# Loras moved between the tile products of a hybrid encoder's projection, in 64-column halves

## The chip, the cores and the metric

The kernel runs on one core of one Trainium2 chip. The metric is device time in microseconds (us) of one execution; medians of several runs are compared. All data are 32-bit floats.

## What is computed

The reference is one step of a streaming encoder layer. The part that matters here is the input side of the token mixer, for 2048 prompt tokens and 8 x 16 sample tokens (17 tiles of 128):

```python
h = rmsnorm(x, w) * (1 + sc1) + sh1          # sc1, sh1 and four more rows from silu(c) @ w_ada + b_ada
proj = h @ w_in                              # q, f, i, gate of the HGRN2 heads; r, k, v of the RWKV-7 heads
dh = shift_right(h, h_prev) - h              # the previous token's row, less this one's
xw, xa, xg = h + dh * mu[0], h + dh * mu[1], h + dh * mu[2]
w_pre = w0 + tanh(xw @ w1) @ w2              # w1: 1024 x 64
a = sigmoid(a0 + (xa @ a1) @ a2)             # a1: 1024 x 64
g = sigmoid(xg @ g1) @ g2                    # g1: 1024 x 128, g2: 128 x 512
```

Behind it stand two recurrences over the tokens, an output product, a router and a mixture of 32 experts.

## The kernel before, in words

`project` (L131) is the first of four parts that run one after another (`project`, `recur`, `merge`, `experts`). Each engine has its own program there, and all order between them is written out with semaphores (`ev(name)`). It has three stages.

**First stage, the tile loop** (TensorE L461 to L472, ScalarE L618 to L625, VectorE L814 to L826). For tile m, TensorE turns tile m+1 (`turn`, L425: eight transposes into banks 0 and 1), multiplies tile m by the 512 columns of i (`i_columns`, L435: eight products of 128 x 512, two instructions each, since a 32-bit product takes two passes; banks 2 and 3 in turn) and then does one of sixteen steps of the late modulation (`late_modulation`, L447, four products of 32 columns side by side into bank 4; `modulation`, L412). ScalarE and VectorE each scale and shift half of the turned tile into `hT` (`keep_h`, L600 and L789), prepare tile m+2 (`norm`, L587 and L782), and ScalarE copies the i product of tile m-1 to `stage` (`keep_i`, L609). POOL loads the modulation's weights two ahead (L266 to L274), and before the ninth of them the three lora weights `lora_w` (L268 to L271). SyncE loads x and stores i.

**Second stage, the loras.** It has 40 steps (g, k): five groups g (four of 512 tokens, one of the 128 sample tokens) by eight blocks k of 128 features. For a step n = 8 g + k, ScalarE writes three copies of h times (1 - mu) (`scale_h`, L630), VectorE adds the previous token's h times mu to each (`mix_h`, L828), and TensorE multiplies the three by w1, a1 and g1 and sums over k in PSUM (`lora`, L479). The mixed data have three buffers (`mixed`, L189), so scaling of step n waits until TensorE is done with step n-3 (L634). The two 64-column products go beside each other into one bank, the 128-column one into another, and two pairs of banks take turns by group:

```python
            def lora(g, k):
                low, high = (P[5], P[6]) if g % 2 == 0 else (P[7], P[4])
                for j in range(2):
                    eng.matmul(low[64 * j:64 * j + 64, 0:w], lora_w[:, k, 64 * j:64 * j + 64], mixed[:, n % 3, j, 0:w], start=(k == 0), stop=(k == KD - 1))
                eng.matmul(high[:, 0:w], lora_w[:, k, 128:256], mixed[:, n % 3, 2, 0:w], start=(k == 0), stop=(k == KD - 1)).then_inc(ev("mixed_used"), 1)
```

When a group is summed, ScalarE moves its two banks to `te` (`keep_lora`, L642: two sigmoids and a copy), VectorE turns the first into a tanh (L841), and TensorE makes the gate g of four tiles (`gate`, L490, one product of 128 x 512 each, banks 2 and 3 in turn) behind k = 5 and 6 of the next group. ScalarE copies all 17 gates to the two buffers of `stage` (`keep_gate`, L651), each when SyncE's store of the gate two before it has landed (`store_gate`, L361). TensorE waits for the last of these copies (L513 to L516) and goes on to the third stage.

**Third stage, the pairs** (L538): 20 pairs of a 128-feature block c and 448 tokens, with products for r, k, v, q and f and, for the first 13, one tile of the output gate with `wt`. POOL loads `wt` and the first five weight blocks `wc` in this order once the first stage is done (L275 to L282).

## Time and profile before

| | |
|---|---|
| median of three runs | 2957.2 us (2951.2 to 2960.57) |
| the profiled execution's own time | 2960.53 us |
| its span, first to last instruction | 2958.6 us |
| TensorE (PE) busy | 2727.0 us, 92% |
| VectorE (DVE) busy | 1521.0 us, 51% |
| ScalarE (ACT) busy | 847.7 us, 29% |
| GpSimd (POOL) busy | 351.7 us, 12% |
| mean granted TensorE clock | 0.968 of full speed |

The profiled execution is 3.3 us above the median. In the profile, PE is TensorE's products and PEld its weight loads, which run beside them; the ends of products are modelled, so starts are the better measure. A timeline row gives start and length in us, engine, line, operation, output and inputs, shape and count; in brackets the idle time before it and what ended it. Shapes like 128*64 are the rows and columns of TensorE's array that the weights take.

### The profile page before, as it was taken

What the parts mean: (1) busy time and instruction counts of PE and PEld (TensorE: products, weight loads), DVE (VectorE), ACT (ScalarE), POOL (GpSimd) and SP (SyncE); (2) the same over time, 40 slices, a digit from 0 to 9 for tenths busy, and PEclk for the clock granted to TensorE, in tenths of its full rate; (3) what the DMA queues carried; (4) which work ended last, traced back from release to release, by engine and by line L of the source; (5) the groups of instructions that cost most, each with busy time, mean ns of one, the idle gap of its engine ahead of it and who ended that gap; (6) DMA issues with size and microseconds to landing.
All of it is one profiled execution on the core that took longest, in us unless ns stands there. A gap on an engine that the chain in (4) does not pass through costs nothing. (4 is left out here: it accounts for less than half of the span.)

```text
span 2958.6 us, 80057 instructions
## 1 busy us (share of the span) xinstructions
PE 2727.0 (92%) x33313; PEld 1714.7 (58%) x33314; DVE 1521.0 (51%) x3704; ACT 847.7 (29%) x1747; POOL 351.7 (12%) x477
## 2 busy tenths in 40 slices
PE   6998999999999989999999699976999999999988
PEld 2432445455454547887878455543666667666753
DVE  3246356556666656777777445454333333333328
ACT  2347334333444433444444222220000000000006
POOL 0000000000000000211213000001122222222223
PEclk9999999999999989999999799997999999999999
DMA  8641024223232286665563586571798668778768
GB/s 300 215 151 43 31 91 136 92 101 128 101 122 92 94 262 155 163 187 157 151 180 117 171 289 224 221 277 62 274 377 325 238 252 328 277 293 321 294 211 342
DMA packets 307723, 580.29 MB, mean 196 GB/s; under 512 B 56494, under 2 KB 240742, under 8 KB 292168
## 3 DMA queue, kind: packets, MB, share of 16 engines
q1 hardware_dynamic: 257544, 486.12, 46.4%
q0 software_dynamic: 18736, 70.27, 6.7%
q10 hardware_dynamic: 31248, 21.08, 2.4%
q8 instruction: 150, 2.46, 0.3%
q14 instruction: 45, 0.37, 0.0%
HBM read 411.77 MB, written 165.60 MB: 195 GB/s over the span
## 5 line engine op out<-in xcount | busy, mean ns | idle before, releaser
L523 PE MATMUL pj_P<-normed,pj_wc 128*128 128x448 f32 (+2 forms) x1600 | 594.9, 519 | 0.9 <-ACT pj_stage L656 0.9
L2699 PE MATMUL moe_PG<-wgu,moe_xT 128*32 128x256 f32 x9600 | 557.1, 381 | 37.0 <-DVE moe_hid L2553 18.3
L2699 PEld LDWEIGHTS moe_PG<-wgu,moe_xT 128*32 128x32 f32 x9600 | 381.4, 110 | 192.7 <-issue 61.7
L523 PEld LDWEIGHTS pj_P<-normed,pj_wc 128*128 128x128 f32 x1600 | 295.8, 190 | 259.6 <-issue 243.6
L2710 PE MATMUL moe_PTY<-wd,moe_hT 128*32 128x256 f32 x4800 | 295.2, 379 | 4.5 <-DVE moe_hT L2556 4.4
L2598 ACT ACTIVATE moe_sg<-moe_PG 128x128 f32<-128x128 f32 x150 | 41.6, 277 | 828.2 <-PE moe_PG L2699 648.7
L2539 DVE STREAM_TRANSPOSE moe_xT<-moe_xg 128x256 f32<-128x256 f32 x151 | 98.6, 653 | 321.8 <-PE moe_PG L2699 315.6
L2132 PE MATMUL merge_PO<-merge_w,merge_mT 128*128 128x512 f32 x544 | 239.7, 599 | 0.8 <-DMA merge_w<-in_w_out 0.5
L2710 PEld LDWEIGHTS moe_PTY<-wd,moe_hT 128*32 128x32 f32 x4800 | 193.3, 110 | 75.3 <-DVE moe_hT L2556 7.6
L2638 POOL DMA_INDIRECT moe_xg<-scratch_h,moe_row x152 | 148.2, 975 | 570.9 <-DVE moe_xT L2539 562.5
L2132 PEld LDWEIGHTS merge_PO<-merge_w,merge_mT 128*128 128x128 f32 x544 | 102.6, 191 | 125.2 <-issue 124.5
L2535 DVE COPY moe_y<-moe_PTY 128x256 f32<-128x256 f32 x151 | 64.0, 424 | 186.7 <-DMA scratch_y_rows<-moe_y 145.8
L444 PE MATMUL pj_P<-pj_wt,normed 128*128 128x512 f32 x272 | 120.4, 596 | 0.0
L282 POOL DMA_DIRECT2D pj_wc<-in_w_in x20 | 17.6, 883 | 676.7 <-PE pj_P L525 640.0
L554 PE MATMUL pj_P<-pj_wt,normed 128*128 128x512 f32 x208 | 92.7, 599 | 0.0
L1808 DVE COPY_PREDICATED re_Y<-re_const,re_P 128x256 f32<-128x256 uint32 x166 | 64.4, 441 | 52.4 <-PE re_P L1339 49.8
L908 DVE SCALAR_TENSOR_TENSOR pj_lf<-pj_P,pj_z 128x448 f32<-128x448 f32 (+1 forms) x20 | 12.2, 611 | 151.4 <-ACT pj_z L715 151.4
L677 ACT ACTIVATE pj_rk<-pj_P,pj_keep_mu 128x448 f32<-128x448 f32 (+1 forms) x60 | 35.5, 601 | 184.2 <-DVEq L950 91.6
L838 DVE SCALAR_TENSOR_TENSOR pj_hk<-normed,pj_prm,pj_hk 128x512 f32<-128x512 f32 x96 | 65.5, 745 | 39.7 <-ACT pj_hk L639 39.4
L2246 DVE TENSOR_TENSOR merge_x<-merge_PO,merge_maps 128x1024 f32<-128x1024 f32 x17 | 20.8, 1225 | 124.8 <-PE merge_PO L2132 124.8
L444 PEld LDWEIGHTS pj_P<-pj_wt,normed 128*128 128x128 f32 x272 | 50.7, 192 | 58.3 <-issue 58.3
L958 DVE TENSOR_TENSOR pj_hk<-pj_hk 128x224 f32<-128x224 f32 (+2 forms) x240 | 71.6, 375 | 2.9
(428 smaller groups left out, 4007.3 us busy)
## 6 DMA issues: line engine op xcount, KB each, us to landing
wgu<-in_w_gate SPq DMA_DIRECT2D x32, 2048.0 KB
wgu<-in_w_up SPq DMA_DIRECT2D x32, 2048.0 KB
wd<-in_w_down SPq DMA_DIRECT2D x32, 2048.0 KB
scratch_y_rows<-merge_zeros SPq DMA_DIRECT2D x51, 512.0 KB, 5.0
scratch_hk<-pj_hk SPq DMA_DIRECT2D x16, 1344.0 KB, 5.8
normed<-scratch_hk SPq DMA_DIRECT2D x32, 640.0 KB, 8.0
re_hkf<-scratch_hk SPq DMA_DIRECT2D x32, 640.0 KB
scratch_y_rows<-moe_y ACTq DMA_DIRECT2D x604, 32.0 KB
```

The costliest lines, as they stand in the source:

```text
L444: ins = eng.matmul(P[2 + m % 2][:, :], hT_cols(m)[:, k, :], wt[:, k, :], start=(k == 0), stop=(k == KD - 1))
L523: ins = eng.matmul(bank[:, 0:wp], wc[:, j, k, :], hT[:, k, k0:k0 + wp], start=(k == 0), stop=(k == KD - 1), skip_group_check=True)
L554: ins = eng.matmul(PQ[:, :], rows[:, k, :], wt[:, k, :], start=(k == 0), stop=(k == KD - 1))
L838: ins = eng.scalar_tensor_tensor(out, before, prm[:, p:p + 1], out, ALU.mult, ALU.add)
L958: step(eng.tensor_tensor(d, d, s, ALU.mult))
L1808: eng.copy_predicated(every_other(Y[lv - 1], g), level_mask(C_LEVEL_T, lv).bitcast(U32).unsqueeze(1).to_broadcast([128, 4, CH]), heads(src ...
L2132: ins = eng.matmul(PO[:, half, :], mT[:, n % 2, k, :], w[:, k, 512 * half:512 * half + 512], start=(k == 0), stop=(k == KD - 1))
L2535: eng.tensor_copy(y[p][:, :], PY[:, :]).then_inc(ev("y_kept"), 1)
L2539: eng.transpose(xT[:, :, :], xg[p][:, :].rearrange("p (i k) -> p k i", k=KD)).then_inc(ev("xT_made"), 1)
L2638: eng.indirect_dma_start(xg[p][:, :], None, t["h2"].rearrange("t (q c) -> (t q) c", q=4), bass.IndirectOffsetOnAxis(ap=row[:, p:p + 1], ax ...
L2699: ins = eng.matmul(PG[32 * q:32 * q + 32, 0, 0:256].rearrange("p (a b) -> p a b", a=2), xT[:, k, :], wgu[p][:, :, k, 128 * q:128 * q + 128 ...
L2710: ins = eng.matmul(PY[32 * n:32 * n + 32, :], hT[:, k, :], wd[p][:, k, 256 * n:256 * n + 256], start=(k == 0), stop=(k == KE - 1))
```

## The change

- TensorE multiplies by g1 in two halves of 64 columns, so that all four products of a lora step have 64 columns. All four prompt groups use banks 5 and 6, the sample group 7 and 4.
- Steps 0 to 25 of the 40 stand in the tile loop: two behind each tile's product from tile 4 to tile 16. ScalarE scales them in tile m's part behind `keep_i(m - 1)`, VectorE mixes them at the end of its part. Steps 26 to 39 stay behind the loop, scaled and mixed two steps ahead of their use.
- The first two groups are moved to `te` as plain copies at tiles 8 and 12, and their sigmoids are done at once at tile 15 (`squash_early`). Group 2 is moved at tile 16.
- Of the gates, two follow each of the steps 26 to 31, and one each of the last four. Even ones are copied by ScalarE, odd ones by VectorE.
- POOL loads the lora weights ahead of the third modulation load, and the first r weights ahead of the gate weights.

```diff
+        EARLY_GROUPS = LORA_GROUPS - 2
+        EARLY = 512 * EARLY_GROUPS
+        N_LORA = KD * (LORA_GROUPS + 1)
+        FIRST_LATE = 2 * (NT - 4)
...
+        def lora_steps(m):
+            return range(2 * (m - 4), 2 * (m - 4) + 2) if m >= 4 else ()
+
+        def lora_banks(g):
+            return (P[5], P[6]) if g < LORA_GROUPS else (P[7], P[4])
+
+        def lora_gates(n):
+            if n < KD * LORA_GROUPS:
+                return range(2 * (n - FIRST_LATE), 2 * (n - FIRST_LATE) + 2)
+            return range(12 + n - (N_LORA - 4), 13 + n - (N_LORA - 4)) if n >= N_LORA - 4 else ()
+
+        def keep_gate(eng, m):
+            eng.wait_ge(ev("gate_made"), m + 1)
+            p = (NT + m) % 2
+            eng.wait_ge(ev(f"stage_out{p}"), 16 * (len(range(p, NT, 2)) + len(range((NT + p) % 2, m, 2))))
+            src, done = P[2 + m % 2][:, :], ev(f"gate_kept{m % 2}")
+            if m % 2 == 0:
+                eng.copy(stage[:, p, :], src).then_inc(done, 1)
+            else:
+                eng.tensor_copy(stage[:, p, :], src).then_inc(done, 1)
...
-                if n == KD:
+                if n == 2:
                     for j, name in enumerate(("rw_w1", "rw_a1", "rw_g1")):
...
-            eng.dma_start(wt[:, :, :], w_in[:, :, COL_G:COL_G + 512]).then_inc(ev("wt_in"), 16)
             for c in range(4):
                 for j, c0 in enumerate((COL_R, COL_K, COL_V, COL_Q, COL_F)):
+                    if c == 0 and j == 1:
+                        eng.dma_start(wt[:, :, :], w_in[:, :, COL_G:COL_G + 512]).then_inc(ev("wt_in"), 16)
...
+            def lora(n):
+                g, k, w = n // KD, n % KD, 512 if n < KD * LORA_GROUPS else 128
+                eng.wait_ge(ev("mixed_ready"), n + 1)
+                if k == 0 and 0 < g < LORA_GROUPS:
+                    eng.wait_ge(ev("lora_read"), g)
+                if k == 0 and g == LORA_GROUPS:
+                    eng.wait_ge(ev("mod_read"), 3)
+                low, high = lora_banks(g)
+                for j in range(4):
+                    ins = eng.matmul((low, high)[j // 2][64 * (j % 2):64 * (j % 2) + 64, 0:w], lora_w[:, k, 64 * j:64 * j + 64], mixed[:, n % 3, min(j, 2), 0:w],
+                                     start=(k == 0), stop=(k == KD - 1))
+                ins.then_inc(ev("mixed_used"), 1)
...
                 i_columns(m)
+                if m == 4:
+                    eng.wait_ge(ev("lora_in"), 48)
+                for n in lora_steps(m):
+                    lora(n)
...
+            for n in range(FIRST_LATE, N_LORA):
+                lora(n)
+                for m in lora_gates(n):
+                    if m == 0:
+                        eng.wait_ge(ev("lora_squashed"), 1)
+                    if m % 4 == 0 and m >= 4 * EARLY_GROUPS:
+                        eng.wait_ge(ev("lora_read"), m // 4 + 1)
+                    gate(m)
...
+            def keep_lora(g):
+                eng.wait_ge(ev("mixed_used"), KD * g + KD)
+                w, k0 = 512 if g < LORA_GROUPS else 128, 512 * g
+                low, high = lora_banks(g)
+                if g < EARLY_GROUPS:
+                    eng.copy(te[:, 0, k0:k0 + w], low[:, 0:w])
+                    eng.copy(te[:, 1, k0:k0 + w], high[:, 0:w]).then_inc(ev("lora_read"), 1)
+                else:
+                    eng.activation(te[0:64, 0, k0:k0 + w], low[0:64, 0:w], ACT.Sigmoid, scale=2.0)
+                    eng.copy(te[64:128, 0, k0:k0 + w], low[64:128, 0:w])
+                    eng.activation(te[:, 1, k0:k0 + w], high[:, 0:w], ACT.Sigmoid).then_inc(ev("lora_read"), 1)
+
+            def squash_early():
+                eng.wait_ge(ev("lora_read"), EARLY_GROUPS)
+                eng.activation(te[:, 1, 0:EARLY], te[:, 1, 0:EARLY], ACT.Sigmoid)
+                eng.activation(te[0:64, 0, 0:EARLY], te[0:64, 0, 0:EARLY], ACT.Sigmoid, scale=2.0).then_inc(ev("lora_squashed"), 1)
...
                 if m:
                     keep_i(m - 1)
+                if m >= 8 and m % 4 == 0:
+                    keep_lora(m // 4 - 2)
+                for n in lora_steps(m):
+                    scale_h(n)
+                if m == NT - 2:
+                    squash_early()
             keep_i(NT - 1)
+            scale_h(FIRST_LATE)
+            scale_h(FIRST_LATE + 1)
...
+            for n in range(FIRST_LATE, N_LORA):
+                if n + 2 < N_LORA:
+                    scale_h(n + 2)
+                if n == KD * LORA_GROUPS:
+                    keep_lora(LORA_GROUPS - 1)
+                for m in lora_gates(n):
+                    if m % 2 == 0:
+                        keep_gate(eng, m)
...
+                for n in lora_steps(m):
+                    mix_h(n)
+
+            mix_h(FIRST_LATE)
+            mix_h(FIRST_LATE + 1)
+            keep_mod(2)
+            for n in range(FIRST_LATE, N_LORA):
+                if n + 2 < N_LORA:
+                    mix_h(n + 2)
+                for m in lora_gates(n):
+                    if m % 2:
+                        keep_gate(eng, m)
```

## Rows read from the trace of the kernel before

**Rows 1.** The page: busy time of the engines, and TensorE's busy tenths in 40 slices.

```profile
PE 2727.0 (92%) x33313; PEld 1714.7 (58%) x33314; DVE 1521.0 (51%) x3704; ACT 847.7 (29%) x1747; POOL 351.7 (12%) x477
...
PE   6998999999999989999999699976999999999988
```

**Rows 2.** Busy time by stretch: start:end, then busy us of PE, PEld, DVE, ACT, POOL.

```profile
155.99:164.88 8.89, 8.89 (x33) 3.95 (x32) 2.27 (x6) 3.53 (x9) 0.53 (x1) 1.00 0.44 147
190.72:309.76 119.04, 101.24 (x292) 28.91 (x291) 74.96 (x127) 88.57 (x156) 5.28 (x6) 0.90 0.23 78
309.76:900.00 590.24, 586.47 (x1873) 307.97 (x1874) 339.35 (x832) 228.74 (x351) 13.24 (x15) 0.99 0.29 100
```

**Rows 3.** Who waited for whom, 190 to 312 us: total, times, longest.

```profile
DVE pj_hk L838 <- ACT pj_hk L639: 46.3, 13, 16.2
...
PEld pj_P L487 <- DVE pj_hk L838: 28.3, 23, 3.6
```

**Rows 4.** Timeline of ScalarE, then of VectorE: start, length, what, count.

```profile
205.01 6.08 ACT L639 ACTIVATE pj_hk<-normed,pj_keep_mu 128x512 f32<-128x512 f32 x9 [1.08 <-PE pj_P L488]
...
206.99 14.65 DVE L838 SCALAR_TENSOR_TENSOR pj_hk<-normed,pj_prm,pj_hk 128x512 f32<-128x512 f32 x21 [0.95 <-ACT pj_hk L639]
...
292.09 2.63 DVE L838 SCALAR_TENSOR_TENSOR pj_hk<-pj_hT_pad,pj_prm,pj_hk 128x128 f32<-128x128 f32 x9 [5.25 <-ACT pj_hk L639]
```

**Rows 5.** Timeline of TensorE in the loras between gates: start, length, what, count.

```profile
284.90 1.88 PE L497 MATMUL pj_P<-pj_fg,pj_te 128*128 128x512 f32 x4
286.71 1.08 PE L487 MATMUL pj_P<-pj_hk,pj_rk 128*64 128x512 f32 x4
287.71 1.13 PE L488 MATMUL pj_P<-pj_hk,pj_rk 128*128 128x512 f32 x2
288.68 1.88 PE L497 MATMUL pj_P<-pj_fg,pj_te 128*128 128x512 f32 x4
```

**Rows 6.** Timeline of TensorE, one tile of the first stage.

```profile
155.99 1.06 PE L415 MATMUL pj_P<-pj_wc,pj_cT 128*32 128x512 f32 x8
156.99 1.09 PE L432 MATMUL pj_P<-held_ident,pj_rk 128*128 128x128 f32 x8
157.92 7.03 PE L444 MATMUL pj_P<-pj_wt,normed 128*128 128x512 f32 x16
164.88 1.06 PE L415 MATMUL pj_P<-pj_wc,pj_cT 128*32 128x512 f32 x8
```

**Rows 7.** Timeline of TensorE in the experts, packed products.

```profile
2104.14 3.66 PE L2699 MATMUL moe_PG<-wgu,moe_xT 128*32 128x256 f32 x64 [0.82 <-issue]
2107.59 1.94 PE L2710 MATMUL moe_PTY<-wd,moe_hT 128*32 128x256 f32 x32
```

**Rows 8.** Copies of 512 columns out of PSUM, on ScalarE and on VectorE.

```profile
L656 ACT COPY pj_stage<-pj_P 128x512 f32<-128x512 f32 x17 | 9.9, 585 | 17.7 <-PE pj_P L497 17.3 <-DMA scratch_tm<-pj_stage 0.5
...
37.83 0.69 DVE L811 COPY pj_mod_T<-pj_P 128x512 f32<-128x512 f32 x1 [1.27 <-PE pj_P L459]
```

**Rows 9.** Transfers: gate stores; x for tile 4; its turning; POOL's loads, 190 to 215 us.

```profile
DMA to landing us min/median/max: 2.0/2.0/2.0
...
52.45 1.06 ACT L594 ACTIVATE pj_rk<-pj_rk 128x1024 f32<-128x1024 f32 x1 [0.27 <-DMA pj_rk<-in_x_prompt]
...
68.10 1.09 PE L432 MATMUL pj_P<-held_ident,pj_rk 128*128 128x128 f32 x8
...
q0 software_dynamic: 1248, 4.72, 59.1%
```

**Rows 10.** Timeline of TensorE at the end of the loras, and two stretches.

```profile
293.02 0.44 PE L487 MATMUL pj_P<-pj_hk,pj_rk 128*64 128x128 f32 x4 [0.40 <-DVE pj_hk L838]
...
300.38 3.16 PE L497 MATMUL pj_P<-pj_fg,pj_te 128*128 128x512 f32 x4
...
299.30:303.40 4.10, 4.08 (x10) 1.80 (x10) 1.69 (x6) 1.37 (x4) 0.00 (x0) 0.58 0.00 0
309.76:317.63 7.87, 7.87 (x16) 3.69 (x17) 0.00 (x0) 0.00 (x0) 0.00 (x0) 0.78 0.09 33
```

More of the change, by code:

```diff
@@ L361, in store_gate @@
             def store_gate(m):
-                eng.wait_ge(ev("gate_kept"), m + 1)
+                eng.wait_ge(ev(f"gate_kept{m % 2}"), m // 2 + 1)
                 eng.dma_start(t["tm"][128 * m:128 * m + 128, 1024:1536], stage[:, (NT + m) % 2, :]).then_inc(ev(f"stage_out{(NT + m) % 2}"), 16)
@@ L477, in _ @@
             ins.then_inc(ev("ends_turned"), 1)
-            def lora(g, k):
-                n, w = KD * g + k, 512 if g < LORA_GROUPS else 128
-                eng.wait_ge(ev("mixed_ready"), n + 1)
-                if k == 0 and g >= 2:
-                    eng.wait_ge(ev("lora_read"), g - 1)
-                low, high = (P[5], P[6]) if g % 2 == 0 else (P[7], P[4])
-                for j in range(2):
-                    eng.matmul(low[64 * j:64 * j + 64, 0:w], lora_w[:, k, 64 * j:64 * j + 64], mixed[:, n % 3, j, 0:w], start=(k == 0), stop=(k == KD - 1))
-                eng.matmul(high[:, 0:w], lora_w[:, k, 128:256], mixed[:, n % 3, 2, 0:w], start=(k == 0), stop=(k == KD - 1)).then_inc(ev("mixed_used"), 1)
             def gate(m):
@@ L614, in keep_i, with scale_h @@
                 eng.copy(stage[:, m % 2, :], P[2 + m % 2][:, :]).then_inc(ev("i_kept"), 1)
[L616 to L632 removed]
+            def scale_h(n):
+                g, k, w = n // KD, n % KD, 512 if n < KD * LORA_GROUPS else 128
                 if n >= 3:
@@ L645, in keep_lora @@
                 w, k0 = 512 if g < LORA_GROUPS else 128, 512 * g
-                low, high = (P[5], P[6]) if g % 2 == 0 else (P[7], P[4])
-                eng.activation(te[0:64, 0, k0:k0 + w], low[0:64, 0:w], ACT.Sigmoid, scale=2.0)
-                eng.copy(te[64:128, 0, k0:k0 + w], low[64:128, 0:w])
-                eng.activation(te[:, 1, k0:k0 + w], high[:, 0:w], ACT.Sigmoid).then_inc(ev("lora_read"), 1)
-            def keep_gate(m):
-                eng.wait_ge(ev("gate_made"), m + 1)
-                p = (NT + m) % 2
-                eng.wait_ge(ev(f"stage_out{p}"), 16 * (len(range(p, NT, 2)) + len(range((NT + p) % 2, m, 2))))
-                eng.copy(stage[:, p, :], P[2 + m % 2][:, :]).then_inc(ev("gate_kept"), 1)
@@ L658, in _ @@
-            for g in range(LORA_GROUPS + 1):
-                for k in range(KD):
-                    scale_h(g, k)
-                    if g and k == 2:
-                        keep_lora(g - 1)
-                    if g and k == 7:
-                        for q in range(4):
-                            keep_gate(4 * g - 4 + q)
+                low, high = lora_banks(g)
[6 more added lines that the diff above has]
+                    eng.activation(te[:, 1, k0:k0 + w], high[:, 0:w], ACT.Sigmoid).then_inc(ev("lora_read"), 1)
@@ new lines, in squash_early @@
+            def squash_early():
+                eng.wait_ge(ev("lora_read"), EARLY_GROUPS)
+                eng.activation(te[:, 1, 0:EARLY], te[:, 1, 0:EARLY], ACT.Sigmoid)
+                eng.activation(te[0:64, 0, 0:EARLY], te[0:64, 0, 0:EARLY], ACT.Sigmoid, scale=2.0).then_inc(ev("lora_squashed"), 1)
+            norm(0)
+            norm(1)
+            for m in range(NT):
+                if m < PT:
+                    keep_h(m)
+                if m + 2 < NT:
+                    norm(m + 2)
+                if m:
+                    keep_i(m - 1)
+                if m >= 8 and m % 4 == 0:
[4 more added lines that the diff above has]
+                    squash_early()
@@ L666, in _ @@
             keep_lora(LORA_GROUPS)
-            keep_gate(PT)
+            keep_gate(eng, PT)
             eng.wait_ge(ev("shift_out"), 32)
@@ L805, in keep_h, with mix_h, keep_lora @@
                     ins.then_inc(ev(("hT_dve", "hT_act")[a]), 1)
+            def mix_h(n):
+                g, k = n // KD, n % KD
+                eng.wait_ge(ev("mixed_scaled"), n + 1)
+                for j in range(3):
+                    p = PRM["mu_lora"] + KD * j + k
+                    if g < LORA_GROUPS:
+                        out, before = mixed[:, n % 3, j, :], hT[:, k, 512 * g:512 * g + 512]
+                    else:
+                        out, before = by_stream(mixed[:, n % 3, j, 0:128]), hT_pad[:, k, :, 0:DEC]
+                    ins = eng.scalar_tensor_tensor(out, before, prm[:, p:p + 1], out, ALU.mult, ALU.add)
+                ins.then_inc(ev("mixed_ready"), 1)
+            def keep_lora(name, count, k0, k1):
+                eng.wait_ge(ev(name), count)
+                eng.tensor_scalar(te[0:64, 0, k0:k1], te[0:64, 0, k0:k1], 2.0, -1.0, ALU.mult, ALU.add).then_inc(ev("lora_kept"), 1)
             norm(0)
```

67 lines of the change are left out of this document (15 added, 52 removed).

## The prediction

> **What bounds the kernel now.** I read the page first: TensorE is busy 92% of the span, every other engine at most 51%, and its row of tenths hardly dips below 9 in the projection, the first quarter or so of the span [rows 1]. The change touches the projection's first two stages, so I cut the span there. Three stretches tell them apart [rows 2]. A tile of the first stage lasts 8.89 us, and TensorE works through all of it at full clock, while VectorE works 2.27 us of it and ScalarE 3.53: this stage is bound by TensorE and two engines have room. The second stage (the loras, from the end of the last tile's products at 190.72 to the first product of the channel pairs at 309.76) lasts 119.04 us; TensorE is counted busy 101 of them, but at a mean clock of 0.90, and what it has to do is far less (below). The third stretch, the pairs, is TensorE without a gap again (586.5 of 590.2 us), so its start sets everything after it.
>
> The waits of the second stage say who paces it [rows 3]: TensorE waits for VectorE's mixing in 28.3 us of its weight loads, VectorE waits 46.3 us for ScalarE's scaling, and ScalarE in turn may not scale before TensorE has freed a buffer. It is a ring through three engines with three buffers. The costs of a step are three scalings and three mixings; a run of nine scalings lasts 6.08 us and one of twenty-one mixings 14.65 [rows 4], so 2.03 and 2.09 us per step. 32 wide steps of VectorE alone are 67 us.
>
> **What TensorE pays.** A step now is four 64-column instructions (two products, two passes each), 1.00 us to the next start, and two 128-column ones, 0.97 us to the next start where nothing is waited for [rows 5]. Of plain 128-column products 16 take 6.96 us (157.92 to 164.88), so 0.43 each [rows 6]. Two 64-column products side by side thus cost 2 x 0.43 = 0.86 plus 0.14 (0.15 below), what changing the array's split costs. In halves, all eight instructions of a step have one split. The row nearest to an unbroken packed chain is the experts' 64 instructions of 256 columns, four side by side: 3.45 us to the next start, 16 slots of 0.214, with nothing lost between packs [rows 7]. So I take four slots of 0.43 = 1.72 us per step, two steps in a row 3.44, plus 0.15 for the change of split: **3.6 us per tile**. Upper bound: nothing is hidden between groups of four, 4 x 1.00 = 4.0. Lower bound 3.44.
>
> The Trainium skill (TensorEngine Tiling (Array Packing), Key Properties) says that changing the tiling mode drains TensorE, which speaks against the change: each tile gains a switch, since the modulation behind the loras has 32-column tiles. The modulation takes 1.00 us now for 0.86 of work [rows 6], so rows agree that a switch costs about 0.15; whether one between two packed splits does, no row shows. By the rule the sum stands as I have it; without it I could take off 13 x 0.15 = 2.0 us, an estimate.
>
> **The sum.** Removed: the stretch of 119.04 us.
>
> Added in the tile loop: tiles 4 to 15 lie wholly ahead of 190.72's counterpart, 12 x 3.6 = 43.2 us (41.3 to 48). All of it is on the path, TensorE having no gap there. ScalarE gets 2 x 2.03 = 4.1 us more per tile, 7.6 of 12.5; VectorE 4.2 more, 6.5 of 12.5. Their order hides it: scaling for tile m begins when tile m-1's product is copied, that is 0.7 us after its end, and mixing of the second step is done some 7 us after it, while TensorE needs it 12.5 us after it. At tiles 8 and 16 the single pair of lora banks must first be emptied: ScalarE waits until 3.6 us, copies twice 0.585 [rows 8] (at 16 three such), scales until 9 to 9.5, mixing ends at 11 to 11.6: still ahead of 12.5, by one microsecond only. Ring buffers: the first scaling needs step n-3, long done; the second needs the first lora of tile m-1, done 1.9 us (1.72 + 0.15) after its product. At nothing I cost the early sigmoids and their table load at tile 15 (about 3.5 us of ScalarE, in its idle half).
>
> Tail, from the last tile's product end: loras 24 and 25 3.6, last modulation 1.0, the eight transposes 1.1 = 5.7. Steps 26 and 27 are mixed by then or within a microsecond (scaling from 0.7, mixing ends 4.8 and 6.8). Then six steps, each a lora of 1.72 + 0.15 and two gates of 1.81 together [rows 5] = 3.68, in all 22.1. Beside them ScalarE has 2.03 + 0.585 and VectorE 2.09 + 0.69 (a PSUM copy of that shape [rows 8]), 2.8 at most, so TensorE paces. The stores of the gates: two buffers, a landing of 2.0 us after the issue [rows 9], the same buffer again 3.7 us later: hidden. So 27.8 us.
> Last the eight 128-token steps with gates 12 to 16. Today from the first of them to the pairs it is 16.7 us (293.02 to 309.76), with a stretch in which four gate instructions take 3.16 us in place of 1.88 at a mean clock of 0.58, so mostly at the lower level of 1.2 GHz [rows 10]. VectorE needs 2.63/3 = 0.88 us per step, and on ScalarE the three evacuations of group 3 (3 x 0.585) stand in between. TensorE's own work is eight times about 0.6 and five gates of about 0.95, 9.6; with the chain lora, sigmoid, gate, copy at the end (2.0 us as now) and a wait of about 2 us for the evacuation of group 3, I get 13.8, and 15.3 with one low-clock stretch like today's. I take 15.3 (13 to 18).
> Tail: 5.7 + 22.1 + 15.3 = 43.1 us. The pairs' first product takes 7.87 us today at a mean clock of 0.78, so partly at the 1.2 GHz level [rows 10]; I leave that as it is.
>
> Gain: 119.04 - 43.2 - 43.1 = **32.7 us**.
>
> **What is moved past queues.** POOL: the three lora loads (1 MB) come behind the first two modulation loads, some 85 us earlier than now. They join SyncE's traffic when the engines' queue share is full; the transfer that suffers is x for tile 4, for which ScalarE waits 0.27 us now, until 52.45 [rows 9]. TensorE turns that tile behind tile 2's product, at 68.1 [rows 9], and it is ready some 2.6 us after landing, so about 13 us of slack: no cost; bounds 0 and 4. Later in POOL's queue the third modulation load waits for TensorE anyway. Weights of r now go ahead of the gate weights: the 4.7 MB of both land within the 25 us from 190 on [rows 9], of which they are issued some 2 us in; the pairs will begin some 37 us after the issue, so both orders are hidden. SyncE: gate stores wait for two semaphores by parity in turn, behind 0.5 us of shift stores, at most half a microsecond once.
>
> The profiled execution took 2960.5 us beside a span of 2958.6, 3.3 us above the median of 2957.2. So 2960.5 - 32.7 = 2927.8 for such an execution, and 3.3 less, 2924.5, against the median: I say **2924.5 us**. What a measurement can tell from no change is about 0.3%, 9 us.
>
> **Rivals.**
> (a) Same mechanism, other sizes: chains unhidden (+4.8 in the tiles, +1 in the tail), the bank switch at 8, 12 and 16 stalling 1.5 us each, the x load 4, the tail at a low clock twice (+3). All together 17.3, so 2942; the other way, 3.44 per tile, no low clock, 13.8: 2919. Part of the forecast's 0.85, with its half below 2930.
> (b) The late steps are paced not by TensorE but by the ring again: today the stage takes 119 us for 40 steps without TensorE being full. If each of the six takes 5 instead of 3.7, and the small steps 20 us: +13, 2937. For it: two engines now share the copies and each serves two others. Against: scaling runs two steps ahead. 0.08.
> (c) Nearly no change: the first stage, so far free of waits, gets stalls of 2 us in every tile (12 x 2 = 24). For it: only 1 us of slack at tiles 8 and 16. Against: the other tiles have 5. Then 2949. 0.03.
> (d) Slower: 64-column tiles don't run beside each other where both halves of the gate lora share one moving operand. All 32 wide steps are on the path now. If both pairs fall apart a step costs 3.44 and not 1.72: 55 more, 2979.5; if only the gate halves do, 27.5 more, 2952. It ends slower from 32.7/32 = 1.0 us lost per step. For it: no row has two tiles with the same moving data in this form. Against: the first pair runs in 1.00 us. 0.04, half of it slower, half within 0.3%.
>
> **Numbers.** The range reaches from 2916 (lower bounds with a low measurement) to 2942 (the upper end of (a), which covers (b)). Faster is the forecast with (b), 0.93; (c) and the milder half of (d) are within 0.3%, 0.05; the other half of (d) is slower, 0.02.
>
> **What would show it.** Tile pitch from tile 4 on: 12.4 to 12.6 us, TensorE without a gap, and lora's 16 instructions spanning 3.6. Right for (c) would be waits of lora's weight loads on VectorE's mixing in the tile loop; right for (d) a lora span of 5 us and above. Tail: 43 us from the last tile's product to the first r product, with gates two by two every 3.7 us; (b) shows as waits on mixing there. The pairs, the recurrence and the experts should keep their lengths, so that the whole span falls by what the projection loses. A pair stretch that is longer than now would be a cost that I don't see.

## The result, and the profile after

The changed kernel takes 2941.6 us (median of 12 runs, 2933.9 to 2950.0) where the kernel before takes 2956.7 beside it on the same chip (12 runs, 2951.2 to 2967.0): a ratio of 0.9947, 95% interval 0.9936 to 0.9958. The gain is 15.1 us by the medians and 21.0 by the two profiled executions (spans 2958.6 and 2937.6). The forecast was 32.7. The direction is right, and less than half of the size came; 2941.6 lies at the very edge of the range.

The timeline of TensorE, two tiles of the first stage (start, length, what, count), answers to [rows 6]:

```profile
85.47 3.65 PE L493 MATMUL pj_P<-pj_hk,pj_rk 128*64 128x512 f32 x16
89.05 1.06 PE L442 MATMUL pj_P<-pj_wc,pj_cT 128*32 128x512 f32 x8
90.05 1.09 PE L459 MATMUL pj_P<-held_ident,pj_rk 128*128 128x128 f32 x8
90.97 7.03 PE L471 MATMUL pj_P<-pj_wt,normed 128*128 128x512 f32 x16
97.94 3.65 PE L493 MATMUL pj_P<-pj_hk,pj_rk 128*64 128x512 f32 x16
```

The two loras of a tile take 3.58 us to the next start (85.47 to 89.05), the pitch is 12.47, and no row names a wait. This is the forecast's tile loop. Twelve of these and 0.6 us that the start of the kernel lost (the last group of modulation products ahead of the tile loop begins at 30.57 instead of 29.95) move the end of the last tile's products from 190.72 to 234.31.

The same timeline behind the last tile, up to the first product of the pairs (the idle time ahead of an instruction and what ended it stand in brackets):

```profile
234.31 3.65 PE L493 MATMUL pj_P<-pj_hk,pj_rk 128*64 128x512 f32 x16
...
239.87 1.94 PE L493 MATMUL pj_P<-pj_hk,pj_rk 128*64 128x512 f32 x8
241.74 1.98 PE L531 MATMUL pj_P<-pj_fg,pj_te 128*128 128x512 f32 x4
243.65 1.94 PE L493 MATMUL pj_P<-pj_hk,pj_rk 128*64 128x512 f32 x8
245.52 1.98 PE L531 MATMUL pj_P<-pj_fg,pj_te 128*128 128x512 f32 x4
247.44 1.94 PE L493 MATMUL pj_P<-pj_hk,pj_rk 128*64 128x512 f32 x8
253.73 2.07 PE L531 MATMUL pj_P<-pj_fg,pj_te 128*128 128x512 f32 x2 [4.36 <-ACT pj_stage L279]
256.00 2.08 PE L531 MATMUL pj_P<-pj_fg,pj_te 128*128 128x512 f32 x2 [0.20 <-DVE pj_stage L281]
258.01 2.88 PE L493 MATMUL pj_P<-pj_hk,pj_rk 128*64 128x512 f32 x8
...
270.60 1.09 PE L493 MATMUL pj_P<-pj_hk,pj_rk 128*64 128x128 f32 x16
...
284.37 0.99 PE L555 MATMUL pj_P<-normed,pj_wc 128*128 128x448 f32 x2 [1.02 <-ACT pj_stage L279]
```

The tail is 284.37 - 234.31 = 50.06 us. It splits into 5.56 up to the first late step, six steps up to 270.60, and 13.77 of small steps. An undisturbed step takes 3.78 us (239.87 to 243.65); six would be 22.7, but there are 30.73 between 239.87 and 270.60: **8.05 us are lost**, all of them behind 247.44. The rows name 4.8 us of waits for copies of gates (4.36, 0.20 and 0.23, the last at 261.12); the other 3.3 us are products that take longer, at the lower clock (below).

Who waited for whom between 234 and 286 us (total, times, longest), beside [rows 3]:

```profile
DVE pj_stage L281 <- DMA scratch_tm<-pj_stage: 14.3, 4, 7.7
ACT pj_stage L279 <- DMA scratch_tm<-pj_stage: 12.7, 2, 7.8
...
PEld pj_P L493 <- DVE pj_hk L860: 8.0, 8, 2.1
```

The ring of [rows 3] no longer paces the late steps: of the 8.0 us that weight loads wait for mixing (28.3 before, in all 40 steps), 3.0 lie in the six steps, where no product waits for it; in the small steps products still wait 0.59, 1.89 and 0.22 us. In the six steps both copying engines wait for the **stores of the gates** to land. The landing times of these 17 stores were 2.0/2.0/2.0 before [rows 9]; the same view of the changed kernel, and the share of the queues in two stretches of 5 us (245 to 250, then 255 to 260; packets, MB, share of the 16 engines):

```profile
DMA to landing us min/median/max: 2.0/2.0/9.0
```

```profile
q0 software_dynamic: 413, 1.63, 94.6%
q1 hardware_dynamic: 89, 0.11, 6.3%
...
q0 software_dynamic: 146, 0.51, 35.4%
q1 hardware_dynamic: 281, 0.51, 28.1%
```

q0 is POOL's queue with the 4.7 MB of weights. Before, these loads were over at 215 us and the first gate was stored at 236; now POOL issues them when the last modulation products (237.90) are done, and the first gate store goes out at 245.7, into them. From 260 on q0 is silent, and stores land in 2.0 us again.

The busy time by stretch (columns as in [rows 2]): the tail, the stall in it, the end of that stall, and the first product of the pairs:

```profile
234.31:284.37 50.06, 41.55 (x179) 14.33 (x179) 26.80 (x56) 27.52 (x60) 5.29 (x6) 0.93 0.52 183
247.40:262.00 14.60, 9.81 (x23) 2.72 (x23) 3.77 (x7) 3.95 (x7) 0.00 (x0) 0.77 0.76 266
...
255.00:260.00 5.00, 4.79 (x9) 1.26 (x10) 2.68 (x4) 0.52 (x1) 0.00 (x0) 0.50 0.63 204
...
284.37:290.62 6.25, 6.25 (x18) 2.98 (x18) 0.00 (x0) 0.00 (x0) 0.00 (x0) 1.00 0.18 68
```

The pairs start at 284.37 instead of 309.76, 25.4 us earlier, and their first product runs at full clock: 6.25 us in place of 7.87, at a granted clock of 1.00 in place of 0.78 [rows 10]. So the first g product is 27.1 us earlier (291.5, before 318.6). Of these the kernel ends only 21.0 us earlier: **6.1 us are lost behind the projection**, in parts whose work the change doesn't touch. I cut the span behind the first g product by starts of TensorE's products (us): to the last product of the bonus; from the recurrence's first score product to the first of its solve; from there to the last score product; from the last solve product to the first of the merge; from the first to the last gate and up product of the experts. What lies between these pieces is in the whole rest alone:

| profiled execution | start of g | to bonus end | joint to recurrence | recurrence | joint to merge | experts | whole rest |
|---|---|---|---|---|---|---|---|
| before | 318.6 | 760.5 | 11.9 | 514.0 | 62.0 | 830.1 | 2640.0 |
| after | 291.5 | 761.3 | 14.4 | 514.0 | 64.6 | 830.7 | 2646.1 |

Here 5.1 of the 6.1 us lie in the two joints (2.5 and 2.6), none in the recurrence and 0.6 in the experts.

### The profile page after: what moved, and what is told of

It is laid out like the page before. It is cut to its first block and busy times, and to the rows that moved or that the text cites. A ratio compares the mean times of both kernels' runs of the same rounds, so it can differ in the third digit from the quotient of the medians.

```text
span 2937.6 us, 80216 instructions
## 1 busy us (share of the span) xinstructions
PE 2701.2 (92%) x33393; PEld 1697.0 (58%) x33394; DVE 1522.7 (52%) x3711; ACT 842.3 (29%) x1739; POOL 352.0 (12%) x477
## 5 line engine op out<-in xcount | busy, mean ns | idle before, releaser
L2751 PEld LDWEIGHTS moe_PG<-wgu,moe_xT 128*32 128x32 f32 x9600 | 372.2, 110 | 202.3 <-issue 64.5
L2762 PEld LDWEIGHTS moe_PTY<-wd,moe_hT 128*32 128x32 f32 x4800 | 187.3, 110 | 79.4 <-DVE moe_hT L2608 9.3
L1657 ACT COPY re_XT<-re_P 128x256 f32<-128x256 f32 x132 | 42.7, 375 | 108.5 <-PE re_P L1399 108.5
```

The lines of the kernel that those rows point to most:

```text
L2751: ins = eng.matmul(PG[32 * q:32 * q + 32, 0, 0:256].rearrange("p (a b) -> p a b", a=2), xT[:, k, :], wgu[p][:, :, k, 128 * q:128 * q + 128 ...
L2762: ins = eng.matmul(PY[32 * n:32 * n + 32, :], hT[:, k, :], wd[p][:, k, 256 * n:256 * n + 256], start=(k == 0), stop=(k == KE - 1))
```

## The experiments

They ran in five groups; the kernels of a group shared one chip and the runs of the kernel before on it, and groups one and four ran on the same chip. Ratios are to the kernel before of the same group. Two questions were open: is the tail's loss really POOL's loads meeting the stores, and what takes time behind the projection?

### First group: the tail, and the halves (kernel before 2962.5 us)

**hold**: POOL's loads wait until eleven gates are made.

```diff
             eng.wait_ge(ev("i_done"), NT)
+            eng.wait_ge(ev("gate_made"), 11)
```

> The changed kernel, with POOL's six weight loads for the pairs (4.7 MB) held back until gate 10 is made. Theory L (the tail is 7 us too long because the gates' stores share the transfer engines with these loads): the stores land in 2.0 to 2.7 us again, no copy waits for a store longer than 1 us, and the tail, from the last tile's product to the first r product, falls from 50.1 us to 43 to 44. The r weights are issued some 31 us into it and land 5 us later, so the pairs start without waiting; the gate weights and k's may come a little late (0 to 3 us in the pairs' first). Rival S (the copies wait because SyncE issues four modulation stores and two shift stores ahead of the first gate store): these stay, and the tail only falls to 47 or stays at 50. Rival V (ScalarE and VectorE pace the late steps, and the stores only hide it): stores land quickly, and the tail stays above 48 with TensorE waiting for mixing.

Measured: 2943.8 us, ratio 0.9934 (0.9921 to 0.9948), tail 49.36. The timeline of ScalarE's copies in it:

```profile
247.08 0.58 ACT L279 COPY pj_stage<-pj_P 128x512 f32<-128x512 f32 x1 [1.35 <-PE pj_P L532]
...
250.86 0.59 ACT L279 COPY pj_stage<-pj_P 128x512 f32<-128x512 f32 x1 [1.35 <-PE pj_P L532]
...
279.45 0.59 ACT L279 COPY pj_stage<-pj_P 128x512 f32<-128x512 f32 x1 [6.89 <-DMA scratch_tm<-pj_stage]
```

Gates 0 to 11 now come two by two every 3.78 us, and their copies wait for TensorE alone: the six steps take 22.69 us (30.73 in the changed kernel), so nothing is lost in them. The loads then go out from 262.8 on, and it is the last gates that wait, 6.89 us on ScalarE and 7.5 on VectorE; the small steps take 21.11 us in place of 13.77. The stall follows the loads: the mechanism is shown, but this edit only moves its cost, and the tail of 43 to 44 that I expected of it didn't come.

**four**: the loads stay early, and the gates go to four buffers (two more are borrowed from the pairs' tiles, idle at that time).

```diff
+        def gate_rows(m):
+            return (stage[:, 1, :], stage[:, 0, :], z[:, :], lf[:, :])[m % 4]
...
-                eng.copy(stage[:, p, :], src).then_inc(done, 1)
+                eng.copy(gate_rows(m), src).then_inc(done, 1)
```

> The changed kernel, with the gates copied to four buffers in turn (the two of the stage and two tiles that are idle until the pairs) in place of two. Theory L: the first stores land as late as before (7 to 9 us), but gates 2 and 3 need not wait for them; gates 4 and 5 wait some 2 us each. Tail 44 to 46 us in place of 50.1. Rival S: the first store is issued as late as now, which with four buffers matters as little: same number, so this run does not tell L from S, only the wait for buffers from rival V (tail stays at 50).

Measured: 2939.5 us, ratio 0.9913 (0.9896 to 0.9930); tail **43.0**, pairs at 277.71. The only wait for a copy that is left to a product of TensorE in the six steps is this one:

```profile
255.02 1.12 PE L544 MATMUL pj_P<-pj_fg,pj_te 128*128 128x512 f32 x2 [0.42 <-DVE pj_stage L294]
```

With a place to put the gates, the tail is 7 us shorter, although copies still wait up to 2.67 us for a store to land. That it meets the forecast of 43.1 is luck in its parts: 5.55, 23.71 and 13.74 us where 5.7, 22.1 and 15.3 were forecast.

**full_g1**: the changed kernel with the gate lora in one 128-column product.

```diff
-                for j in range(4):
-                    ins = eng.matmul((low, high)[j // 2][64 * (j % 2):64 * (j % 2) + 64, 0:w], lora_w[:, k, 64 * j:64 * j + 64], mixed[:, n % 3, min(j, 2), 0:w],
-                                     start=(k == 0), stop=(k == KD - 1))
+                for j in range(2):
+                    eng.matmul(low[64 * j:64 * j + 64, 0:w], lora_w[:, k, 64 * j:64 * j + 64], mixed[:, n % 3, j, 0:w], start=(k == 0), stop=(k == KD - 1))
+                ins = eng.matmul(high[:, 0:w], lora_w[:, k, 128:256], mixed[:, n % 3, 2, 0:w], start=(k == 0), stop=(k == KD - 1))
```

> The changed kernel, with g1 multiplied in one product of 128 columns, as before the change, in place of two halves; all else as changed. Theory (changing the array's split costs 0.15 us, twice more per step): a tile's two loras take 4.0 to 4.2 us in place of 3.58, so 13 tiles are 6 to 8 us longer, and the late steps 0.15 each; in the tail this hides in the waits for stores. Total 6 to 8 us more than the changed kernel. Rival (halves bring nothing, since the products of two passes are the same work): 3.6 us per tile and no difference.

Measured: 2949.3 us, 0.9944 (0.9927 to 0.9961). TensorE in a tile:

```profile
98.00 1.08 PE L493 MATMUL pj_P<-pj_hk,pj_rk 128*64 128x512 f32 x4
99.01 1.12 PE L494 MATMUL pj_P<-pj_hk,pj_rk 128*128 128x512 f32 x2
100.07 1.08 PE L493 MATMUL pj_P<-pj_hk,pj_rk 128*64 128x512 f32 x4
101.08 1.12 PE L494 MATMUL pj_P<-pj_hk,pj_rk 128*128 128x512 f32 x2
102.13 1.06 PE L442 MATMUL pj_P<-pj_wc,pj_cT 128*32 128x512 f32 x8
```

4.13 us per tile against 3.58, so halves save 0.55 per tile; the last tile's products end 6.1 us later (240.39), and the pairs start 8.2 us later (292.6). The array's share of the work is the same in both forms (four slots of 0.43 a step); what the halves save is three changes of split per tile, 0.18 us each. The 6 to 8 us more in total that I expected aren't shown: the ratio is that of the changed kernel (0.9947, on another chip).

**halves_only**: the kernel before with the halves alone.

> The kernel before, with g1 multiplied in two halves of 64 columns and nothing else changed. Theory (the ring through ScalarE and VectorE paces the second stage): the stage of 119.0 us shortens by 0 to 3 us although TensorE's work for a step falls from 2.0 to 1.87. Rival (TensorE paces it): 0.2 to 0.4 us less in each of 40 steps, so 8 us or more.

Measured: 2966.8 us, 1.0011 (0.9997 to 1.0025), with a stage of 116.18 us (119.04 before). It was run again in the third group:

> The kernel before with g1 in halves, repeated: its first run was slower than before by 4 us by the medians though its pairs begin 2.8 us earlier. Theory R: this time 0 to 4 us faster than b_third. Theory P' in the form that 80 more instructions in TensorE's stream make the rest longer: 2 to 6 us slower than b_third again.

Again 1.0020 (1.0007 to 1.0033), 2959.7 us. The second stage took 113.93 us where b_third (the kernel before, same chip) has 115.78, but its first stage ended 2.2 us later (193.2 for 191.0), so the pairs start at about the same time (307.1 and 306.8); the rest of the span is 2644.3 where b_third has 2634.4. A projection no longer than before, with a slower kernel: that is the second question.

### Second and third group: does an earlier end stay a gain? (before 2951.8 and 2954.5)

**a_again, a_third** are the changed kernel and **b_again, b_third** the kernel before, unchanged, run as candidates themselves.

> The changed kernel once more, unaltered. By its first trace the pairs begin 25.4 us earlier than before, by its first twelve runs the whole is only 15 us shorter. Theory R (what lies behind the projection varies from execution to execution by several us, and the first comparison fell on its short side): projection again 284 to 285 us; the ratio to before comes out nearer to 1 - 25/2957 = 0.9915. Theory P (moving the rest in time, or another program in front of it, makes the rest some 8 us longer): the ratio stays near 0.9947.

> The kernel before, unaltered, compared with itself: what the comparison says of no change. Both theories: 1.000 within 0.0015. Its trace is a second look at the part behind the projection: theory R expects it to differ from the first look (2648.8 us from the first product of the pairs to the end) by 3 to 10 us, theory P expects 2645 to 2652.

> The changed kernel a third time, on one chip beside the kernel before, the halves and the four buffers, all in the same role. Theory R (the part behind the projection only varies): from the first product of the gate columns in the pairs to the end it takes what the kernel before takes, within 3 us of medians, and the changed kernel is 25 to 27 us faster than b_third. Theory P' (something of the change makes the rest longer): it takes 6 to 10 us more again, and the changed kernel is 16 to 20 us faster than b_third.

> The kernel before once more, as the yardstick for the three runs beside it. Compared with the shared runs of itself: 1.000 to 1.0015 (the second look gave 1.0014, which bounds how far such a comparison is off by itself). The part behind the projection, by the trace: 2630 to 2640 us from the first product of the gate columns in the pairs.

| | us | ratio (interval) | g start | recurrence | experts | rest |
|---|---|---|---|---|---|---|
| b_again | 2955.0 | 1.0014 (1.0005 to 1.0024) | 318.3 | 511.0 | 823.9 | 2630.2 |
| a_again | 2937.3 | 0.9955 (0.9938 to 0.9972) | 292.1 | 517.5 | 823.9 | 2642.6 |
| b_third | 2952.7 | 0.9997 (0.9986 to 1.0007) | 315.6 | 511.0 | 824.4 | 2634.4 |
| a_third | 2935.9 | 0.9937 (0.9920 to 0.9955) | 291.3 | 517.2 | 824.6 | 2644.4 |

The kernel before against itself gives up to 1.0014, so this is what a ratio here can be off by. The gain of the change is stable (0.9937 to 0.9955), and a loss behind comes each time: the rest is 12.4 and 10.0 us longer in these pairs. Of that, the recurrence has 6.5 and 6.2 us, the joint to the merge 3.5 and 2.0 (65.0 in both, for 61.5 and 63.0); the experts have nothing.

**b_shift**: the kernel before, with sixteen chained copies on ScalarE ahead of the last gate's copy, so that all that follows starts later.

```diff
+            for i in range(16):
+                eng.copy(z[:, :], hT[:, 0, 1:513]).then_inc(ev("pad"), 1)
+                eng.wait_ge(ev("pad"), i + 1)
             keep_gate(PT)
```

> The kernel before, with sixteen copies on ScalarE, each waiting for the one before, put ahead of the last gate's copy: TensorE stands still for some 10 to 14 us more before the pairs and nothing else changes. Theory R: the time grows by just what the pairs' start moves (read from the trace, some 12 us), 2 us either way. Theory P (a shift alone costs): it grows by 5 us or more beyond that.

Measured: 2966.8 us, 1.0054 (1.0041 to 1.0067). The first g product comes 10.0 us later than in b_again, and the time rises by 11.8 us. So what the projection loses passes through to the end of the kernel; nothing behind it takes a late start up. Against the shared runs of the kernel before the rise is 15.0 us, and the profile's rest is 6.6 us longer than b_again's (2636.8 for 2630.2) although TensorE's program is that of the kernel before: a single profile of one kernel can be off by that much, or a shift costs something of its own, and this run can't tell which. Whether an early start stays a gain, it can't say either.

**four_order** and **four_order_again**: four buffers, and the four modulation stores behind the gate stores on SyncE.

```diff
-            store_mod(2)
+            held_back = lambda: store_mod(2)
...
             for m in range(NT):
                 store_gate(m)
+            held_back()
```

> The changed kernel with four gate buffers and, besides, the last four stores of the modulation behind the gate stores on SyncE's queue. In the run with four buffers a tail of 43.0 us still had waits of 2.7, 2.7, 1.7, 0.9 and 1.5 us of copies for stores. Rival S: the first gate store is issued some 1.3 us earlier, so the tail is 1 to 1.5 us shorter, 41.5 to 42. Theory L (sharing with POOL's loads is all there is): the landing is set by the loads' end, 43 within 0.4. The total is that of four buffers within 2 us.

> The changed kernel with four gate buffers and the modulation's last stores behind them, repeated. Tail 43 us in place of 50. Theory R: 6 to 8 us faster than a_third and 31 to 33 faster than b_third. Theory P': 5 to 12 faster than a_third, since the rest varies, and 25 to 30 faster than b_third.

Measured: 2925.8 us, 0.9921 (0.9907 to 0.9934), and 2924.6 us, 0.9902 (0.9887 to 0.9917); tails 43.16 and 44.47. The order of the stores does take away what was left of the stall: no product waits for a copy in the six steps, which last 22.69 us in both runs (23.71 in four). The small steps give it back, 14.91 and 16.23 us in place of 13.74, in a stretch at the lower clock that four did not have (268 to 270 us in four_order_again: granted clock 0.50). a_third, the changed kernel itself, has such a stretch in its small steps too (15.09 us), behind a wait of 1.91 us:

```profile
273.34 2.00 PE L493 MATMUL pj_P<-pj_hk,pj_rk 128*64 128x128 f32 x16 [1.91 <-DVE pj_hk L860]
```

In a_again, whose product waited 1.90 us at the same place, the next eight instructions took 0.66 us and no such stretch came (13.77 us): one program has it in one execution and not in another. Beside a_third on one chip, four_order_again is 11.3 us faster.

### Fourth and fifth group: the length of TensorE's program (before 2963.3 and 2956.0)

The halves add 80 weight loads and 80 products (compare the page's counts, [rows 1] and x33393), 160 instructions, ahead of the recurrence, which is written out in TensorE's program, and of the experts, which are loops in it. These kernels add nothing but empty semaphore increments on TensorE, which no engine waits for: two behind each of the 40 lora steps (b_pad80, a_pad80, four_order_pad80), six (b_pad240), or 16 in the first four steps and 12 in the others (b_pad496):

```diff
+                for _ in range(2):
+                    eng.sem_inc(ev("pad"), 1)
```

> The kernel before with two semaphore increments behind each lora step in TensorE's stream, 80 in all, and no other work. Theory C (the part behind the projection depends on where its instructions lie or how long the program in front is, not on what the change computes): that part gets 4 to 10 us longer than in b_fourth, as it did with g1 in halves, which also added 80 instructions. Theory R (it only varies): within 3 us of b_fourth by the medians. The projection itself: 0 to 3 us longer.

> The same with six increments behind each step, 240 in all. Theory C: the part behind the projection differs from b_fourth's by some us, in either direction, as another position gives another value. Theory R: within 3 us of b_fourth. The projection: 0 to 8 us longer, where the increments stand in TensorE's way.

> The changed kernel with two semaphore increments behind each lora step, 80 in all. Theory C: the part behind the projection differs from the 2642 to 2646 us that three looks at the changed kernel gave, by 4 us or more, most likely downwards. Theory T (the change's timing, not its code, makes that part longer): it stays at 2642 to 2646. Projection: some 0.1 us per increment in the tile loop, 2 to 6 us longer.

> The kernel before as the yardstick of these three. Ratio to itself 0.999 to 1.0015; from the first gate product of the pairs to the end 2630 to 2640 us.

> The kernel before with 496 semaphore increments in TensorE's stream. So far the experts' part took 817 and 819 us in the two programs whose TensorE stream is 240 instructions longer than before's, and 824 to 836 in all with 0, 80 or 160 more. Theory C256 (what counts is the position of TensorE's loops in its code, in steps of 256 instructions): 496 is 240 once more, so the experts take 817 to 820 us again and the end is some 14 us ahead of the kernel before. Theory C (position, but with another step): any value from 817 to 836. Theory R (chance): 824 to 836. The projection may be 0 to 15 us longer for the increments.

> The changed kernel with four gate buffers, the modulation's last stores behind them, and two semaphore increments behind each lora step, which makes TensorE's stream 240 instructions longer than before's. Theory C256: both gains add up: tail 43 to 44 us, experts 817 to 820, some 7 us less than the changed kernel with the increments alone (ratio 0.9882), so a ratio to before of 0.985 to 0.987. Theory R: 0.990 to 0.992, as without the increments.

| | added against before | us | ratio (interval) | pairs start | joint to merge | experts | rest |
|---|---|---|---|---|---|---|---|
| b_fourth | 0 | 2962.3 | 0.9992 (0.9977 to 1.0006) | 309.7 | 63.2 | 834.0 | 2647.9 |
| b_pad80 | 80 | 2963.9 | 1.0006 (0.9993 to 1.0019) | 310.0 | 66.3 | 831.7 | 2647.3 |
| b_pad240 | 240 | 2948.1 | 0.9949 (0.9931 to 0.9968) | 308.7 | 62.0 | 818.6 | 2632.0 |
| a_pad80 | 160 + 80 | 2926.9 | 0.9882 (0.9862 to 0.9901) | 283.1 | 62.3 | 817.2 | 2631.2 |
| b_pad496 | 496 | 2956.0 | 0.9993 (0.9983 to 1.0003) | 315.1 | 62.5 | 816.9 | 2630.7 |
| four_order_pad80 | 160 + 80 | 2921.3 | 0.9883 (0.9868 to 0.9898) | 276.0 | 63.2 | 816.4 | 2628.8 |

The experts' products in the profiles of b_fourth and b_pad240 (one chip; duration least/median/most in ns, first and last start in us):

```profile
L2699 PE MATMUL moe_PG<-wgu,moe_xT x9600: 376/379/636, 2039.0 to 2873.0; 128*32 128x256 f32 x196
```

```profile
L2701 PE MATMUL moe_PG<-wgu,moe_xT x9600: 376/379/632, 2034.7 to 2853.3; 128*32 128x256 f32 x196
```

The same 9600 products, each as long as before, are done in 818.6 us instead of 834.0. Waits of TensorE from 2030 to 2850 us, b_fourth, then b_pad240:

```profile
PEld moe_PG L2699 <- issue: 65.2, 82, 2.4
```

```profile
PEld moe_PG L2701 <- issue: 55.9, 81, 2.3
```

A part of it (9.3 us) is time in which TensorE's weight loads waited for nothing that the profile shows.

What follows:
- Empty instructions in the projection's code make the kernel before 0.5% faster, without changing what is computed; the pairs start only 1.0 us earlier (308.7 for 309.7), the first g product 2.6, and of the 15.9 us that the rest is shorter than in b_fourth, 15.4 are in the experts. Of the 20 profiles of this study, the four with 240 or 496 added have 816.4 to 818.6 us of experts; the other sixteen (0, 80 or 160 added) have 823.9 to 835.9. On the chip of groups one and four alone it is 817.2 and 818.6 against 831.7 to 835.9 in six profiles. The other two short ones are of group five.
- At **equal length** (counted in products, weight loads and increments) the change loses nothing behind the projection: b_pad240 and a_pad80, both 240 above the kernel before, have rests of 2632.0 and 2631.2. There the change gives 25.6 us at the start of the pairs, 26.4 us of span, and 21.1 by the medians (2948.1 to 2926.9). So an early start can stay a gain; it is one profile of each, and the medians keep 21.1 of the 25.6. What the 240 took away, though, is time in the experts, which the change had never lengthened (823.9 and 823.9, 824.4 and 824.6, 830.1 and 830.7 us). That the length of the program is also what makes the recurrence and the joints longer in the changed kernel isn't shown.
- b_pad496 had the short experts too, but its time didn't fall: 496 increments cost 5.3 us in the lora chain (pairs at 315.1 against 309.8 in the profile of before), and no profile of the kernel before exists on that chip, so what remains can't be told apart. From that kernel's median there (2956.0, less 1.9 to the span, less 318.4 as in b_fourth) its rest would be some 2636 us, an estimate; b_pad496 has 2630.7, so on this chip added instructions may be worth 5 us and not 15.
- 80 more bought nothing (b_pad80). Whether it is a position relative to some block (240 and 496 differ by 256) or merely a matter of 240 and above, these runs can't say. Nor does length explain all: the recurrence took 517 us in a_again and a_third but 512 in four_order and four_order_again, whose TensorE program is as long.

The best version is four_order_pad80 with 2921.3 us, 34.7 below the kernel before beside it and ahead of the changed kernel's ratio by 0.6%. The 0.985 to 0.987 that I expected if both gains added up didn't come: its ratio is no better than a_pad80's (0.9883 and 0.9882) although its pairs start 7 us earlier, 0.24% of the time. They ran on different chips, and the kernel before differs from itself by up to 0.14%; whether that or a smaller effect of the added instructions on this chip hides the 7 us stays open.

## Why the prediction was right or wrong

**The tile loop: right.** 3.6 us per tile were forecast and 3.58 measured, pitch 12.47 within 12.4 to 12.6, no wait of a lora on mixing. full_g1 shows what the halves bring: with a 128-column product between the packed ones, the same slots cost 4.13, for three more changes of split. The switches of the split do cost what [rows 6] had led to: 3.58 is the unbroken chain of 3.44 plus 0.14. The Trainium skill (TensorEngine Tiling (Array Packing), Key Properties) says that changing the tiling mode drains TensorE; this case agrees, with 0.14 us for this change and 0.18 for each of the three in full_g1. Not foreseen: 0.6 us at the start; I put it down to the three lora loads that come earlier on POOL, which wasn't tested, and the last tile's products end anywhere from 233.6 to 235.0 us in the other profiles with this tile loop (full_g1 aside). Rivals (b), (c) and (d) fell: no product of the six late steps waits for mixing, there is no stall in the tiles, and halves that share one moving operand run side by side. That 2941.6 still lies inside the range is luck: of the costs that (a) adds up to 2942 only a stretch at the lower clock came, and it came behind a stall that (a) doesn't have.

**The tail: wrong by 7.0 us** (50.06 for 43.1). The step that failed is "The stores of the gates: two buffers, a landing of 2.0 us after the issue [rows 9], the same buffer again 3.7 us later: hidden." I took the landing from rows in which POOL's queue was silent, and two paragraphs later moved the stores to where that queue is full: 2.0 became up to 9.0 us. Both halves were in my own text; they were never put on one time axis. The sizes: 8.05 us lost in the six steps, 0.6 more for them than 22.1 (3.78 each, not 3.68), and 1.5 less for the small steps (13.77, the value without a low clock that I had worked out and not taken; the same program had 15.09 in a_third). Of the 8.05 us, 3.3 are the lower clock behind the stall. hold moved the stall with the loads; four left 1.0 us of it in the six steps, four_order none. The Trainium skill (DMA: Bandwidth & Descriptors, Arbitration) says that each DMA engine takes packets from its queues in turn; this case agrees in that q0 and q1 both move in each stretch between 245 and 260 us. Equal turns it doesn't show: q0 moved 413 packets to q1's 89 from 245 to 250 us, with 94.6% of the engines, while the first store was on its way. "So both orders are hidden" was right for those who wait for the weights, and said nothing of those who share the engines with them.

**The pairs' first product:** I left it at 7.87; it fell to 6.25, which up to the first g product is a gain of 1.7 that I hadn't counted. In this profile neither the small steps' stretch at 0.58 nor the 0.78 behind it [rows 10] came back. The second did not go because of the first: a_third and a_pad80 had a stretch at the lower clock in the small steps, and their pairs' first product took 6.25 us all the same. It is not the change alone that brings the 6.25 either: the four profiles of the kernel before have 7.9 us in this product's row, but b_pad240, b_pad496 and halves_again, whose loras stand where they stood, have 6.25. What decides it wasn't tested.

**Behind the projection: wrong.** "The pairs, the recurrence and the experts should keep their lengths" cost 6.1 us in the profiled pair and 12.4 and 10.0 in the repeated ones. I had written that a longer part would be a cost that I don't see, and it is. The failed step is that sentence: the joints around the recurrence got longer in all three pairs and the recurrence itself in the repeated two, the experts in none. What makes them longer stays open. The number of instructions ahead in TensorE's program moves the length of the experts (b_pad240 against b_fourth), and at 240 above the kernel before the two kernels' rests are alike; but kernels of one length differ by 6 us in the recurrence, and the kernel before itself has rests of 2630.2, 2634.4, 2640.0 and 2647.9 us in its four profiles, so the 6.1 us of one pair is no firm number.

**The sum** of the profiled pair: 32.7 - 0.4 (tiles and start) - 7.0 (stores) + 1.7 (first product) - 6.1 (behind) = 20.9, measured 21.0. This accounts for the profiled pair alone. The medians say 15.1: the profiled execution of the changed kernel (2939.4) was 2.2 under its median and that of before 3.8 above (2960.5 for 2956.7), together 6.0.

## What to carry to other kernels

A landing time read from a trace holds for the queues as they were in that stretch: whoever moves a store must look up what the DMA engines carry at its new time, and give it buffers by the landing there, not by the old one. A stage that starts earlier can meet a load that used to be over; two more buffers, borrowed from tiles that were idle, were worth 7 us here. Differences of half a per cent can also come from the number of instructions in an engine's program ahead of a loop, so a change of that size should be judged at equal length, or with a padded copy of the old kernel beside it.

## What the runs showed of the hardware that was not expected

- A 256 KB store lands in 2.0 us alone and in up to 9.0 us beside a 4.7 MB load of another queue, at 350 to 375 GB/s for both.
- TensorE was idle for 4.36 us (up to 253.73), and the granted clock fell: 0.50 from 255 to 260 us, the 1.2 GHz level. The eight instructions of a lora took 2.88 us instead of 1.94. A stall can cost more than its length: 4.8 us of waits came with 3.3 us of slower products.
- With 240 empty semaphore increments on TensorE in the projection, the experts, 1700 us later, are 15 us shorter (834.0 to 818.6 us on one chip), with each product as long as before, and the median of the kernel falls by 14.2 us.
- The same program gives experts of 824 us on two chips (groups two and three) and of 834 on another (group four), so such lengths are compared on one chip only.
